# Storing the high and low part of each activation piece side by side, with every high part at a multiple of 256 bytes

## The chip, the cores and the metric

The kernel runs on one core of a Trainium2 chip. Its time is the device time of that core in microseconds (us), as the median of several executions. A profile is one further execution, recorded by the hardware. In it PE is TensorE's matmuls, PEld TensorE's weight loads, DVE is VectorE, ACT is ScalarE, POOL is GpSimd and SP is SyncE. All times are us unless marked ns.

## The reference, cut to what matters

The kernel is one step of an encoder with two layers over 576 tokens (512 of a prompt and 64 of a running stream) of width 1024. Each layer is a SwiGLU feed-forward block, a mixer (pooling in the first layer, an mLSTM in the second) and another feed-forward block:

```python
def _swiglu(u, w_in, w_out):
    h = u @ w_in
    a, b = h[..., :D_FF], h[..., D_FF:]          # D_FF = 2816
    return (jax.nn.silu(a) * b) @ w_out

x = x + 0.5 * _swiglu(_rmsnorm(x, norm_ffn1[i]), ffn1_w_in[i], ffn1_w_out[i])
x = x + mixer(_rmsnorm(x, norm_mix[i]))          # pooling or mLSTM
x = x + 0.5 * _swiglu(_rmsnorm(x, norm_ffn2[i]), ffn2_w_in[i], ffn2_w_out[i])
```

All data is float32. Everything that the change touches is the operand `u` of `u @ w_in`.

## The kernel before, in words

**Precision.** A float32 matmul is done as three passes of fp32r matmuls: each operand is split into a high part (rounded to fp32r) and a low part (the rest), and `passes` (line 1822) gives weight high x data high, weight high x data low, weight low x data high. The weight is the stationary operand and is loaded anew for each matmul, the data is the moving operand of 288 columns (`HALF`, half of the tokens), and so 288 x 4 = 1,152 bytes of each partition are streamed.

**Products.** `u @ w_in` is computed by a Strassen-like scheme with seven products M1 to M7 for each of 11 pairs of output tiles, in each of the two phases of each of the four feed-forward blocks ffn_a to ffn_d. Each product has one of seven combinations of quarters of u as its data. They lie in `u7[kp, part, piece]` with four contraction tiles kp, two parts (high, low) and seven pieces. `PIECES` and `MOVING` (lines 40 to 41) give the piece: M1 has piece 0, M5 1, M2 2, M3 3, M7 4, M6 5 and M4 6. `product_mm` (line 1835) issues one product, here called a **unit**: 4 kp x 3 passes = 12 matmuls in a row on PE, always in the order high, low, high of the data (and weight high, high, low). `product_orders` (line 44) is the order in which PE takes the units; from pair 3 on it repeats M1, M5, M4, M6, M2, M3, M7. `product_waits` puts two semaphore waits ahead of each unit. In the first phase of a block, the first units are interleaved kp by kp.

**Addresses.** A partition's memory is laid out by a running pointer, `region` (line 142). In this build x starts at byte 16,512, which is 128 above a multiple of 256, and takes 72 x 256 bytes, so that `u7` starts at 128 above a multiple of 256 as well. A piece is 1,152 bytes, 4.5 x 256. So in the kernel before a high part starts 128 above a multiple of 256 where its piece is even (M1, M2, M7, M4) and at a multiple of 256 where it is odd (M5, M3, M6), and its low part, seven pieces further, lies the other way round. Below these are the **128-first** and the **0-first** units. The weights `w_hi` and `w_lo` start 128 above a multiple of 256, and each weight tile is 2 x 256 bytes. The `h` tiles (the hidden layer, data of the output product, line 1832) start at a multiple of 256, the second half of the tokens 1,152 bytes behind the first.

**Who fills u7.** ACT writes each high part (`u7_high`, line 754) from a float32 copy (`stage`), in three groups of pieces (`PARTS`: 0 to 1, 2 to 3, 4 to 6), and DVE the low part by a subtraction (`u7_low`, line 1272). ACT also splits all weights (`hi`, line 688, L721), and DVE makes their low part (L1223).

**The place where u7 meets something else.** In the mLSTM the mixer's data `um_hi` and `um_lo` lie in the last 36,864 bytes of u7's region. The output projection of the mixer reads them tile by tile; during its last tile, PE counts `u_free` up after each of seven contraction steps. `u7_high` of ffn_d for kp 2 and 3 therefore waits for `u_free`, and DVE's low parts of kp 1 too (line 1758).

Of the kernel before, what the change touches and what calls it, by code (L numbers as in the profile page):

```python
# [3 lines left out]
P = 128  # L4
D_MODEL = 1024
DT = D_MODEL // P
KP = DT // 2
SEQ, DEC_SEQ = 512, 64
TOK = SEQ + DEC_SEQ
HALF = TOK // 2  # L10
# [121 lines left out]
U_POOL, U_M, U_MOUT, U_END = AT["pool", 0], AT["gates",], AT["mout", 0], len(KEYS)  # L132


def encoder_step(nc, a):
    F32, F32R = mybir.dt.float32, mybir.dt.float32r
    ALU, ACT = mybir.AluOpType, mybir.ActivationFunctionType


    place = [(nc.sbuf_base + 63) // 64 * 64]  # L140

    def region(size):
        offset = place[0]
        place[0] += (size + 63) // 64 * 64
        assert place[0] <= nc.sbuf_usable_end, place[0]
        return offset

    def sb(name, shape, dt=F32, at=None):
        size = 4
        for s in shape[1:]:  # L150
            size *= s
        return nc.alloc_sbuf_tensor_at(name, shape, dt, offset=region(size) if at is None else at)

    x = sb("x", [P, DT, TOK])


    u_at = region(KP * 2 * 7 * HALF * 4)
    u7 = sb("u7", [P, KP, 2, 7, HALF], F32R, at=u_at)
    up_at = u_at + KP * 2 * 7 * HALF * 4 - 2 * DT * U_STRIDE * 4
    up_hi = sb("up_hi", [P, DT, U_STRIDE], F32R, at=up_at)  # L160
    up_lo = sb("up_lo", [P, DT, U_STRIDE], F32R, at=up_at + DT * U_STRIDE * 4)
# [103 lines left out]
    def halves(ap):  # L265
        return ap.rearrange("p (h n) -> p h n", h=2)

    def f32(ap):
        return ap.bitcast(F32)
# [24 lines left out]
    hi_split, lo_split, unit_used = sem("hi_split"), sem("lo_split"), sem("unit_used")  # L294
# [124 lines left out]
    with block as block:  # L419
# [255 lines left out]
        def _(act):  # L675
# [78 lines left out]
            def u7_high(f, kp, part):  # L754

                if part == 1:
                    act.activation(u7[:, kp, 0, 2:4, :], halves(x[:, 2 * kp + 1, :]), ACT.Copy,
                                   scale=ngains[:, f.norm, 2 * kp + 1:2 * kp + 2]).then_inc(u7_hi[1], 1)
                    return
                act.wait_ge(sums_made[part // 2], KP * f.i + kp + 1)  # L760
                first, end = PARTS[part]
                src = stage(f, kp)[:, first:end, :] if part else even_stage(f, kp)
                act.activation(u7[:, kp, 0, first:end, :], src, ACT.Copy) \
                    .then_inc(u7_hi[part], 1)

            def square_tile(j):
# [347 lines left out]
            def mix_square(j):  # L1114

                act.wait_ge(x_ready, 5 * DT + j + 1)
                if j == 0:
                    act.wait_ge(norm_psum, 5)
                elif j > 1:
                    act.wait_ge(mix_added, j - 1)  # L1120
                act.activation((sq if j else sumsq)[:, :], x[:, j, :], ACT.Square).then_inc(mix_squared, 1)

            for j in range(DT - 1):
                ahead(U_MOUT + j)
                act.wait_ge(x_ready, 5 * DT + j + 1)
                if j % 2 == 0:
                    negs_even(ffn_d, j // 2)
                else:
                    negs_odd(ffn_d, j // 2)
                if j in (1, 3):  # L1130
                    for part in range(3):
                        u7_high(ffn_d, j // 2, part)
                mix_square(j)
            act.wait_ge(u_free, 4)
            u7_high(ffn_d, 2, 0)
            u7_high(ffn_d, 2, 1)
            u7_high(ffn_d, 3, 0)
            act.wait_ge(u_free, 6)
            u7_high(ffn_d, 2, 2)
            upto(ffn_d.unit(0, "M7", 0))  # L1140
            act.wait_ge(x_ready, 6 * DT)
# [54 lines left out]
        def _(dve):  # L1196
# [75 lines left out]
            def u7_low(f, kp, part):  # L1272

                dve.wait_ge(u7_hi[part], KP * f.i + kp + 1)
                first, end = PARTS[part]
                src = stage(f, kp)[:, first:end, :] if part else even_stage(f, kp)
                dve.tensor_tensor(u7[:, kp, 1, first:end, :], src,  # L1277
                                  f32(u7[:, kp, 0, first:end, :]), ALU.subtract).then_inc(u7_made[part], 1)

            def add_last(norm):  # L1280

# [540 lines left out]
        def _(pe):  # L1822
            def passes(u, kk, m_h, m_l):

                w = slice(PLACE[u] + kk * P, PLACE[u] + (kk + 1) * P)
                return (w_hi[:, w], m_h), (w_hi[:, w], m_l), (w_lo[:, w], m_h)
# [9 lines left out]
            def product_mm(f, ph, prod, n, kp):  # L1836

                u = f.unit(ph, prod, n)
                dst = r_bank(n) if prod in ("M5", "M3") else q_bank(f, ph, n) if prod == "M2" else p_bank(n)
                piece = PIECES.index(MOVING[prod])  # L1840
                for p, (w, m) in enumerate(passes(u, kp, u7[:, kp, 0, piece, :], u7[:, kp, 1, piece, :])):
                    mm = pe.matmul(dst, w, m, start=prod in ("M1", "M2", "M5") and kp == 0 and p == 0,  # L1842
                                   stop=kp == KP - 1 and p == 2,
                                   skip_group_check=prod in ("M3", "M4", "M6", "M7"))
                if kp == KP - 1:
                    mm.then_inc(unit_used, 1)
# [510 lines left out]
```

## Time and profile before

| | |
|---|---|
| time, median of 3 runs | 1896.24 (1896.02 to 1899.24) |
| span of the profiled execution (first to last instruction) | 1892.5 |
| what lies around the span, taken against the median | 3.7 |
| PE busy | 1871.9 (99% of the span) |
| DVE, ACT, POOL busy | 1254.4, 869.7, 329.9 |
| matmuls on PE | 13,850 |
| of these with u7 as data (L1842) | 7,392 |
| mean granted TensorE clock, share of full speed | 0.997 |

The profiled execution's own time is not recorded apart from its span; the 3.7 us are the difference to the median of the runs, the start and the end of the program. A matmul's duration in the profile, 297 ns, is its time through the pipeline; matmuls overlap, and what counts is the distance between the starts of two neighbours, some 132 to 134 ns.

### The profile page before, as it was taken

The numbers are of one execution on the slowest core, as the hardware profiler recorded it, in microseconds if no ns is written. First come the engines' busy times: TensorE is split into PE (matmuls) and PEld (weight loads), VectorE is DVE, ScalarE is ACT, GpSimd is POOL, SyncE is SP. The second block draws the span as 40 slices with busy tenths as digits, with TensorE's granted clock in tenths as the row PEclk, the third lists the DMA queues.
The fourth block names the chain that finished last, engine by engine and source line by source line (L and its number), as shares of the span: only waits on it lengthen the run. The fifth ranks groups of instructions, "written<-read, shape, count | busy, mean of one in ns | idle before, by whom it ended". The sixth has DMA issues, their size and how long they took to land.

```text
span 1892.5 us, 34440 instructions
## 1 busy us (share of the span) xinstructions
PE 1871.9 (99%) x13850; PEld 1851.5 (98%) x13850; DVE 1254.4 (66%) x1999; ACT 869.7 (46%) x1518; POOL 329.9 (17%) x352
## 2 busy tenths in 40 slices
PE   8999999999999999999999999999999999999998
PEld 8999999998999999999999999999989999999998
DVE  7874487668874488678853786463446888448843
ACT  7652355347652355345532553232434665235532
POOL 2220122121220122132201221300010322012112
PEclk9999999999999999999999999999999999999999
DMA  8773576324773576347644763221113576357632
GB/s 208 162 151 102 125 165 151 107 86 96 161 154 99 125 165 151 106 102 167 144 131 101 171 142 96 90 100 68 57 45 107 118 173 145 102 122 166 130 93 81
DMA packets 116831, 234.71 MB, mean 124 GB/s; under 512 B 13185, under 2 KB 15249, under 8 KB 116673
## 3 DMA queue, kind: packets, MB, share of 16 engines
q1 hardware_dynamic: 77440, 160.59, 27.8%
q0 software_dynamic: 38208, 69.42, 22.3%
q8 instruction: 111, 1.82, 0.4%
q10 hardware_dynamic: 1024, 2.49, 0.4%
q14 instruction: 48, 0.39, 0.1%
HBM read 228.92 MB, written 3.53 MB: 123 GB/s over the span
## 4 chain that ended last, share of the span: by engine, by line
PE 93%; DVE 4%; ACT 2%; DMA 1%; issue 1%; DVEq 0%; ACTq 0%
PE ps L1842 49%; PE ps L1832 39%; DVE w_lo L1223 1%; PE ps L1887 1%; DMA raw_y<-in_ffn_in 1%; PE ps L2159 1%; PE ps L2225 0%; DVE u L1277 0%; PE ps L2162 0%; DMA x<-in_x 0%; PE ps L2024 0%; PE ps L2149 0%; ACT w_hi L721 0%; DVE rstd L1294 0%; PE ps L2134 0%
## 5 line engine op out<-in xcount | busy, mean ns | idle before, releaser
L1842 PE MATMUL ps<-u,w_hi 128*128 128x288 f32 x4928 | 991.9, 297 | 9.5 <-DVE w_lo L1223 4.5
L1842 PEld LDWEIGHTS ps<-u,w_hi 128*128 128x128 f32 x4928 | 794.5, 189 | 13.9 <-DVE w_lo L1223 6.8
L1842 PE MATMUL ps<-u,w_lo 128*128 128x288 f32 x2464 | 729.5, 296 | 0.0
L1842 PEld LDWEIGHTS ps<-u,w_lo 128*128 128x128 f32 x2464 | 464.1, 188 | 0.0
L1832 PE MATMUL ps<-h_lo,w_hi 128*128 128x288 f32 x1386 | 297.9, 296 | 0.0
L1832 PE MATMUL ps<-h_hi,w_hi 128*128 128x288 f32 x1386 | 297.8, 296 | 0.0
L1832 PE MATMUL ps<-h_hi,w_lo 128*128 128x288 f32 x1386 | 297.8, 296 | 0.0
L721 ACT ACTIVATE w_hi<-w_raw 128x768 fp32r<-128x768 f32 (+3 forms) x164 | 136.4, 838 | 319.4 <-PE ps L1832 255.7
L1223 DVE TENSOR_TENSOR w_lo<-w_raw,w_hi 128x768 fp32r<-128x768 f32 (+3 forms) x164 | 167.9, 1032 | 164.2 <-ACT w_hi L721 162.0
L1832 PEld LDWEIGHTS ps<-h_hi,w_hi 128*128 128x128 f32 x1386 | 223.1, 189 | 0.0
L1832 PEld LDWEIGHTS ps<-h_hi,w_lo 128*128 128x128 f32 x1386 | 222.8, 189 | 0.0
L1832 PEld LDWEIGHTS ps<-h_lo,w_hi 128*128 128x128 f32 x1386 | 222.7, 189 | 0.0
L583 POOL DMA_DIRECT2D raw_y<-in_ffn_in x88 | 76.1, 872 | 805.6 <-DVE raw_z L1229 797.6
L721 ACT ACTIVATE w_hi<-raw_y 128x512 fp32r<-128x512 f32 x176 | 110.2, 633 | 181.0 <-PE ps L1842 87.3
L721 ACT ACTIVATE w_hi<-raw_z 128x512 fp32r<-128x512 f32 x176 | 111.2, 633 | 109.1 <-PE ps L1842 68.2
L1223 DVE TENSOR_TENSOR w_lo<-raw_z,w_hi 128x512 fp32r<-128x512 f32 x176 | 121.2, 689 | 51.0 <-ACT w_hi L721 50.2
L1223 DVE TENSOR_TENSOR w_lo<-raw_y,w_hi 128x512 fp32r<-128x512 f32 x176 | 122.9, 700 | 40.9 <-ACT w_hi L721 34.8
L1223 DVE TENSOR_TENSOR w_lo<-raw_a,w_hi 128x512 fp32r<-128x512 f32 x132 | 90.9, 688 | 36.1 <-ACT w_hi L721 36.1
L1832 PE MATMUL ps<-um_hi,w_hi 128*128 128x288 f32 x512 | 113.8, 304 | 0.6 <-DVE q_t L1576 0.4
L575 POOL DMA_DIRECT2D raw_x<-in_ffn_in x88 | 94.5, 1074 | 97.6 <-DMA raw_x<-in_ffn_in 96.3
L1832 PE MATMUL ps<-um_hi,w_lo 128*128 128x288 f32 x512 | 109.6, 296 | 0.0
L1832 PE MATMUL ps<-um_lo,w_hi 128*128 128x288 f32 x512 | 109.5, 295 | 0.0
(268 smaller groups left out, 2125.1 us busy)
## 6 DMA issues: line engine op xcount, KB each, us to landing
raw_a<-in_ffn_in SPq DMA_DIRECT2D x132, 256.0 KB, 4.2
w_raw<-in_ffn_out SPq DMA_DIRECT2D x64, 384.0 KB, 3.1
raw_y<-in_ffn_in SPq DMA_DIRECT2D x88, 256.0 KB, 3.6
raw_x<-in_ffn_in SPq DMA_DIRECT2D x88, 256.0 KB, 2.6
raw_x<-in_ffn_in POOLq DMA_DIRECT2D x88, 256.0 KB, 6.4
raw_y<-in_ffn_in POOLq DMA_DIRECT2D x88, 256.0 KB, 4.9
raw_z<-in_ffn_in POOLq DMA_DIRECT2D x88, 256.0 KB, 4.9
w_raw<-in_ffn_out SPq DMA_DIRECT2D x64, 320.0 KB, 3.0
```

What stands on the lines that cost most here:

```text
L575: pool.dma_start(raw_x[g % 2][:, :], f.w_in[ph * PAIRS + n, 3, :, :], accum_op=ALU.add) \
L583: pool.dma_start(raw_y[g % 2][:, :], f.w_in[ph * PAIRS + n, 2, :, :], accum_op=ALU.add) \
L721: act.activation(w_hi[:, PLACE[u]:PLACE[u] + cols], src, ACT.Copy).then_inc(hi_split, 1)
L1223: dve.tensor_tensor(w_lo[:, PLACE[u]:PLACE[u] + cols], src, f32(w_hi[:, PLACE[u]:PLACE[u] + cols]), ALU.subtract).then_inc(lo_split, 1)
L1832: mm = pe.matmul(ps[:, bank + h, 0:HALF], w, m[:, h * HALF:(h + 1) * HALF], start=first and p == 0, stop=last and p == 2)
L1842: mm = pe.matmul(dst, w, m, start=prod in ("M1", "M2", "M5") and kp == 0 and p == 0, stop=kp == KP - 1 and p == 2, skip_group_check=prod i ...
L1887: mm = pe.matmul(ps[:, 6 + h, 0:HALF], mean_w[:, :], sq8[:, j, h * HALF:(h + 1) * HALF], start=i == 0, stop=i == DT - 1, skip_group_check= ...
L2159: mm = pe.matmul(ps[0:L, 4 + h, 0:DV + 1], probs[0:L, h, c0:c0 + L], v_one[0:L, c, h, :], start=True, stop=c == 0)
```

## The change

`u7` becomes `[kp, piece, part]`, so that a piece's high and low part lie side by side: 2 x 1,152 = 9 x 256 bytes for each piece. The region is moved up by 128 bytes to a multiple of 256. Every high part of all seven pieces then starts at a multiple of 256, and every low part 128 above one. A second `align` moves the next region (raw weights, and with it all that follows) to 128 above a multiple of 256, which is its residue before; in all it moves up by 256 bytes. The `um` and `up` tiles (data of the mixers), which end with u7's region, move up by 128 bytes.

With the new layout other parts of u7 share memory with `um`, so ACT's writes for ffn_d are put in another order with other waits.

```diff
+    def align(size, residue=0):
+        place[0] += (residue - place[0]) % size
+
+    align(256)
+    u_at = region(KP * 7 * 2 * HALF * 4)
+    u7 = sb("u7", [P, KP, 7, 2, HALF], F32R, at=u_at)
+    align(256, 128)
...
-                act.activation(u7[:, kp, 0, first:end, :], src, ACT.Copy) \
+                act.activation(u7[:, kp, first:end, 0, :], src, ACT.Copy) \
...
-                    for part in range(3):
+                    for part in range(3 - j // 2):
                         u7_high(ffn_d, j // 2, part)
                 mix_square(j)
+            act.wait_ge(u_free, 2)
+            u7_high(ffn_d, 1, 2)
             act.wait_ge(u_free, 4)
             u7_high(ffn_d, 2, 0)
-            u7_high(ffn_d, 2, 1)
             u7_high(ffn_d, 3, 0)
             act.wait_ge(u_free, 6)
+            u7_high(ffn_d, 2, 1)
+            act.wait_ge(unit_used, U_MOUT + DT)
             u7_high(ffn_d, 2, 2)
...
-                dve.tensor_tensor(u7[:, kp, 1, first:end, :], src,
-                                  f32(u7[:, kp, 0, first:end, :]), ALU.subtract).then_inc(u7_made[part], 1)
+                dve.tensor_tensor(u7[:, kp, first:end, 1, :], src,
+                                  f32(u7[:, kp, first:end, 0, :]), ALU.subtract).then_inc(u7_made[part], 1)
...
-                for p, (w, m) in enumerate(passes(u, kp, u7[:, kp, 0, piece, :], u7[:, kp, 1, piece, :])):
+                for p, (w, m) in enumerate(passes(u, kp, u7[:, kp, piece, 0, :], u7[:, kp, piece, 1, :])):
```

The order of instructions on PE, DVE, POOL and SP is the same as before; only ACT's differs, at the end of the mLSTM. There, on ACT, before (u_50 is u7, stage_76 the float32 pieces of kp 1; x_ready counts the residual's tiles):

```order
L751 ACTIVATE stage_76<-x,ngains 128x576 [waits x_ready]
L763 ACTIVATE u_50<-stage_76 128x576 [waits sums_even_made]
L757 ACTIVATE u_50<-x,ngains 128x576
L763 ACTIVATE u_50<-stage_76 128x864 [waits sums_odd_made]
L1121 ACTIVATE sq<-x 128x576 [waits mix_added,x_ready]
L721 ACTIVATE w_hi<-raw_y_61 128x512 [waits unit_used,a11_landed0]
```

And now:

```order
L756 ACTIVATE stage_76<-x,ngains 128x576 [waits x_ready]
L768 ACTIVATE u_50<-stage_76 128x2x288 [waits sums_even_made]
L762 ACTIVATE u_50<-x,ngains 128x2x288
L1126 ACTIVATE sq<-x 128x576 [waits mix_added,x_ready]
L726 ACTIVATE w_hi<-raw_y_61 128x512 [waits unit_used,a11_landed0]
```

The write of the last three pieces of kp 1 (128x864) has left this place. A little later on ACT, during the projection's last tile, before (stage_77 and stage_78 are kp 2 and 3):

```order
L1121 ACTIVATE sq<-x 128x576 [waits mix_added,x_ready]
L763 ACTIVATE u_50<-stage_77 128x576 [waits sums_even_made,u_free]
L757 ACTIVATE u_50<-x,ngains 128x576
L763 ACTIVATE u_50<-stage_78 128x576 [waits sums_even_made]
L763 ACTIVATE u_50<-stage_77 128x864 [waits sums_odd_made,u_free]
```

And now:

```order
L1126 ACTIVATE sq<-x 128x576 [waits mix_added,x_ready]
L768 ACTIVATE u_50<-stage_76 128x3x288 [waits sums_odd_made,u_free]
L768 ACTIVATE u_50<-stage_77 128x2x288 [waits sums_even_made,u_free]
L768 ACTIVATE u_50<-stage_78 128x2x288 [waits sums_even_made]
L762 ACTIVATE u_50<-x,ngains 128x2x288 [waits u_free]
L768 ACTIVATE u_50<-stage_77 128x3x288 [waits sums_odd_made,unit_used]
L726 ACTIVATE w_hi<-raw_y_61 128x512 [waits unit_used,s3_summed0]
```

The write for kp 1 stands here now, two writes for kp 2 and 3 have changed places, and the last write of kp 2 waits for the end of the whole projection (unit_used) where it waited for its sixth step. Behind it stands the split of the weight of M7.

## Rows read from the trace of the kernel before

**Rows 1.** The page: busy time, share of the span and instructions of each engine.

```profile
PE 1871.9 (99%) x13850; PEld 1851.5 (98%) x13850; DVE 1254.4 (66%) x1999; ACT 869.7 (46%) x1518; POOL 329.9 (17%) x352
```

**Rows 2.** The page: the chain that ended last, by engine and line.

```profile
PE 93%; DVE 4%; ACT 2%; DMA 1%; issue 1%; DVEq 0%; ACTq 0%
PE ps L1842 49%; PE ps L1832 39%; DVE w_lo L1223 1%; PE ps L1887 1%; DMA raw_y<-in_ffn_in 1%; PE ps L2159 1%; PE ps L2225 0%; DVE u L1277 0%; PE ps L2162 0%; DMA x<-in_x 0%; PE ps L2024 0%; PE ps L2149 0%; ACT w_hi L721 0%; DVE rstd L1294 0%; PE ps L2134 0%
```

**Rows 3.** Groups of PE instructions: count, busy us, mean ns, idle before.

```profile
L1842 PE MATMUL ps<-u,w_hi 128*128 128x288 f32 x4928 | 991.9, 297 | 9.5 <-DVE w_lo L1223 4.5 <-DVE u L1277 3.5 <-ACT side L799 0.7
L1842 PE MATMUL ps<-u,w_lo 128*128 128x288 f32 x2464 | 729.5, 296 | 0.0
```

**Rows 4.** PE's waits: who released it, us in total, times, longest.

```profile
PE ps L1842 <- DVE w_lo L1223: 4.5, 2, 3.2
PE ps L1842 <- DVE u L1277: 3.5, 4, 1.9
```

**Rows 5.** Timeline of PE, ffn_b, second phase, units' first matmuls: start, us.

```profile
644.68 0.29 PE L1842 MATMUL ps<-u,w_hi 128*128 128x288 f32 x1
...
646.30 0.29 PE L1842 MATMUL ps<-u,w_hi 128*128 128x288 f32 x1
...
647.88 0.29 PE L1842 MATMUL ps<-u,w_hi 128*128 128x288 f32 x1
...
649.50 0.30 PE L1842 MATMUL ps<-u,w_hi 128*128 128x288 f32 x1
...
651.09 0.30 PE L1842 MATMUL ps<-u,w_hi 128*128 128x288 f32 x1
...
652.67 0.29 PE L1842 MATMUL ps<-u,w_hi 128*128 128x288 f32 x1
...
654.29 0.30 PE L1842 MATMUL ps<-u,w_hi 128*128 128x288 f32 x1
...
655.88 0.30 PE L1842 MATMUL ps<-u,w_hi 128*128 128x288 f32 x1
...
657.46 0.43 PE L1842 MATMUL ps<-u,w_hi 128*128 128x288 f32 x2
...
659.05 0.42 PE L1842 MATMUL ps<-u,w_hi 128*128 128x288 f32 x2
...
660.66 0.43 PE L1842 MATMUL ps<-u,w_hi 128*128 128x288 f32 x2
```

**Rows 6.** Windows of L1842: stretch, us, PE and PEld busy (count), clock, DMA.

```profile
675.05:764.54 89.49, 89.49 (x674) 89.49 (x673) 1.00 0.69 155
```

**Rows 7.** Windows of L1832 (data h) in ffn_b's second output product.

```profile
767.80:838.10 70.30, 70.30 (x528) 70.26 (x527) 1.00 0.33 93
```

**Rows 8.** Windows, all engines: mLSTM's output projection, then ffn_d's four interleaved units.

```profile
1448.98:1492.45 43.47, 43.47 (x325) 43.31 (x325) 32.85 (x42) 23.48 (x35) 12.99 (x12) 1.00 0.36 94
1492.45:1498.85 6.40, 6.40 (x50) 6.33 (x48) 6.13 (x11) 4.33 (x8) 1.02 (x2) 1.00 0.99 177
```

**Rows 9.** PE at the pooling projection (up is its stationary operand): durations min/median/max.

```profile
L2024 PE MATMUL ps<-w_hi,up_hi x40: 278/281/367, 412.6 to 433.6; 128*128 128x256 f32 x32, 128*79 128x256 f32 x8
```

**Rows 10.** Timeline of ACT at the mLSTM's end: start, us, [idle before, releaser].

```profile
1473.05 0.93 ACT L763 ACTIVATE u<-stage 128x864 fp32r<-128x864 f32 x1 [0.18 <-DVE stage L1269]
...
1487.80 0.67 ACT L1121 ACTIVATE sq<-x 128x576 f32<-128x576 f32 x1
1489.45 0.69 ACT L763 ACTIVATE u<-stage 128x576 fp32r<-128x576 f32 x1 [0.98 <-PE ps L1832]
1490.04 0.77 ACT L757 ACTIVATE u<-x,ngains 128x576 fp32r<-128x576 f32 x1
1490.71 1.50 ACT L763 ACTIVATE u<-stage 128x576 fp32r<-128x576 f32 x2
1493.74 0.64 ACT L721 ACTIVATE w_hi<-raw_y 128x512 fp32r<-128x512 f32 x1 [1.54 <-DMA raw_y<-in_ffn_in]
```

**Rows 11.** Timeline of DVE in the same stretch.

```profile
1488.62 2.95 DVE L1277 TENSOR_TENSOR u<-stage,u 128x576 fp32r<-128x576 f32 x2
1492.65 0.76 DVE L1744 TENSOR_TENSOR x<-x,ps 128x576 f32<-128x576 f32 x1 [1.08 <-PE ps L1832]
...
1495.93 0.51 DVE L1265 SCALAR_TENSOR_TENSOR stage<-x,gains,stage 128x288 f32<-128x288 f32 x1
```

More of the change, by code:

```diff
@@ L154, in encoder_step @@
     x = sb("x", [P, DT, TOK])
-    u_at = region(KP * 2 * 7 * HALF * 4)
-    u7 = sb("u7", [P, KP, 2, 7, HALF], F32R, at=u_at)
+    def align(size, residue=0):
[4 more added lines that the diff above has]
+    align(256, 128)
     up_at = u_at + KP * 2 * 7 * HALF * 4 - 2 * DT * U_STRIDE * 4
@@ L756, in u7_high @@
                 if part == 1:
-                    act.activation(u7[:, kp, 0, 2:4, :], halves(x[:, 2 * kp + 1, :]), ACT.Copy,
+                    act.activation(u7[:, kp, 2:4, 0, :], halves(x[:, 2 * kp + 1, :]), ACT.Copy,
                                    scale=ngains[:, f.norm, 2 * kp + 1:2 * kp + 2]).then_inc(u7_hi[1], 1)
```

## The prediction, written before the changed kernel ran

> **What bounds the kernel.** I read the page first. PE is busy for 1871.9 of 1892.5 us [rows 1], and the chain of what ended last runs through PE for 93%: 49% in L1842, the products on u7, and 39% in L1832 [rows 2]. The reader is to see that nothing but PE's own pace is worth much: the whole idle time ahead of L1842's matmuls is 9.5 us [rows 3], and of it only 3.5 us in four waits are for u7 itself [rows 4]. So a change of u7's addresses can act in two ways: on the distance between two matmuls, or on these few waits.
>
> The next view is therefore the timeline of PE, read not by durations (all are 290 to 300 ns) but by the starts of the units. All stand in one stretch without a wait, in the second phase of ffn_b, where the order is M1, M5, M1, M5, M6, M2, M7, M2, M6, M4, M3. The starts are 649.50 (M5), 651.09 (M6), 652.67 (M2), 654.29 (M7), 655.88 (M2), 657.46 (M6), 659.05 (M4) and 660.66 (M3) [rows 5]. So the lengths are:
> - M5 and M6, 0-first units, the second of them behind another 0-first one: 652.67 - 649.50 = 3.17, or 1.585 each.
> - M2 behind M6, a 128-first unit behind a 0-first one: 1.62.
> - M7 behind M2 and M2 behind M7, 128-first behind 128-first: 657.46 - 654.29 = 3.17, 1.585 each.
> - M6 behind M2, 0-first behind 128-first: 1.59.
> - M4 behind M6, 128-first behind 0-first again: 1.61.
>
> The same product, M2, takes 1.62 behind M6 and 1.58 behind M7, with the same PSUM bank to leave and to enter in both cases (M6 and M7 write the same kind of bank). The number of instructions and waits is the same too. What differs is where the data of the unit before ended: M6's last pass reads a high part at a multiple of 256 bytes, M7's one at 128. Three of the four successions run at the fast pace; only 0-first followed by 128-first is slow.
>
> The sizes to one more digit: the five fast units above take 3.17 + 4.76 (654.29 to 659.05) = 7.93, 1.586 each. From M1 of pair 3 at 675.05 to M3 of the last pair at 764.54 there are eight repetitions of the seven units M1, M5, M4, M6, M2, M3, M7 in 89.49 us [rows 6] (672 starts; the count of 674 has two that were still running). One repetition is 11.186. In it M4 (behind M5), M2 (behind M6) and M7 (behind M3) are slow and four units fast: (11.186 - 4 x 1.586) / 3 = 1.614. A slow unit costs 0.028 us more, 12 matmuls at 134.5 ns instead of 132.2.
>
> **The change, part by part.**
>
> *The products.* With all high parts at multiples of 256, every unit is a 0-first one behind a 0-first one. The succession is in the trace (M6 at 651.09, fast). Slow units before: in a second phase M1 of pair 1, M2 and M4 of pair 0, M7 and M4 and M2 and M7 around pairs 1 and 2 (7), 3 in each of the 8 further repetitions (24) and the last M4: 32, times four blocks = 128. In the first phases, where the head differs and other matmuls stand between some units, I count 31, 30, 29 and 29 = 119. Together 247. Gain 247 x 0.028 = 6.9 us.
>
> *The heads.* The first unit of a second phase, behind the h tiles, takes 646.30 - 644.68 = 1.62 [rows 5]; as a 0-first unit I take it at 1.586, 4 x 0.03 = 0.1. The four units that ffn_c and ffn_d interleave alternate strictly between the two residues and take 6.40 us for 48 matmuls, 133.3 ns each [rows 8] (the count of 50 again has two running ones); at 132.2 they gain 0.05 each, 0.1 together.
>
> *The mixer's data.* um moves by 128 bytes, so its first half goes from 128 to 0 and its second from 0 to 128. Its matmuls alternate between the residues in both cases. Before, with the 128 first, they run 43.47 us / 326 = 133.3 ns [rows 8]; h, with the 0 first, runs at 70.30 / 528 = 133.1 to 133.3 [rows 7]. That is the same pace, so I take nothing, with 1,568 x 0.2 ns = 0.3 us to either side. up moves too, as stationary operand of 120 matmuls [rows 9]; the largest difference known here is that of a slow and a fast matmul, 2.3 ns, so 0.3 us to either side and 0 in the sum.
>
> *The residue of what lies above.* All of it moves by 256 bytes and keeps its residue to 256. Within the trace, data tiles lie at 0 and at 256 above multiples of 512 in turn (h from one k to the next), and h's pace of 133.3 is one number; so I take 0. No row has the weights in another place.
>
> *Strided writes.* DVE and ACT now write runs of 288 with a gap. The trace has DVE reading in two pieces (L1744, 0.76 for 576 elements), which costs no more than the continuous subtraction; a strided write it does not have. A tenth more on ACT's and DVE's some 0.75 us each [rows 10, 11], with about six such instructions ahead of each of the four blocks, would be 0.45 us each, 1.8 us, if PE waited for all of it; below nothing there is no reason. The waits for u7 are only 3.5 us in four [rows 4], so I take 0 and keep 1.8 for the range.
>
> *The new order on ACT.* Removed at 1473.05: 0.93 us [rows 10]; ACT then waits elsewhere. It comes back behind the square at 1487.80, so from 1488.5 to 1489.4. Step four of the last projection was seen at 1489.45 (the start of the write that waited for it), so kp 2's first write starts there as before, kp 3's at 1490.04, the next (0.77) when step six is done, at about 1489.45 + 2 x 0.80 = 1491.05, and the last, 0.93 long, at the end of the projection. That end is seen by DVE at 1492.65 [rows 11]. So ACT is free at 1493.6, and the split of M7's weight behind it waited for a DMA until 1493.74: 0.1 us of slack. DVE's kp 1 subtractions start at 1488.62 and end at 1491.57; the second needs ACT's write of 1489.4 and has it in time. DVE's next use of ACT's late work is the 1495.93 row. What is late by x there reaches PE only beyond 1 us. Cost 0, upper bound 1 us.
>
> **Sum.** 6.9 + 0.1 + 0.1 = 7.1. Against the profiled execution, 1892.5 becomes 1885.4; its start and end around the span stay at 3.7, so the median goes from 1896.24 to **1889.1**. Own range: the slow unit's excess may be 0.025 to 0.031 by the rounding of the rows (6.2 to 7.7), unknown costs up to 3: 1887.5 to 1892.4.
>
> **Two rules of the Trainium skill.** The trace has the same product at 1.58 and at 1.62 us. The page "SBUF — State Buffer", section "Who interferes with whom", gives PE two independent read ports, one for the moving operand and one for weight loads, and says "PE and ACT never wait on anyone". By it no address could change PE's pace, and the change would give 0; the trace disagrees with the first half of that in the kernel before. The fastest long pace here is 132.2 ns. The page "TensorE: Matmul & The Clock Gate", section "Back-to-back issue gap", gives N / 2.4 + 2.5 ns, an estimate of 122.5 for 288 columns; no stretch here shows it, and if the new layout reached it for all 7,392 matmuls the gain would be some 80 us.
>
> **The rivals.**
> 1. *No change.* The slow units are slow by their place in the order, not by addresses: M4, M2 and M7 of the repetition stay at 1.614, and the time stays at 1896.2. For it: the longer units there are always the same three products. Against it: M7 and M2 at the head, in another succession, are fast. The page above on SBUF stands on this side.
> 2. *A still faster pace.* The first M5 behind M1 takes 647.88 - 646.30 = 1.58 [rows 5], by rounding 1.57 to 1.59; if it is 1.575, a pace better than 1.586 exists, and if a run of 0-first units settled in it, all 616 units would gain another 0.011, 6.8 us: 1882.3. Against it: M6 behind M5, 0-first behind 0-first as all will be, is at 1.58 to 1.59 [rows 5].
> 3. *Slower.* What is carried from unit to unit is a phase between weight loads and data, and an unbroken run of 0-first units, or the weights 256 bytes higher, keeps the bad one. Then all units take 1.614: the 369 shorter units lose 0.028 each, +10.3, 1906.6. It decides as soon as more units are lengthened to 1.614 than the 247 that are mended. Against it: the passes within a 0-first unit are the same as before, and its entry from another one was fast.
> 4. *Half.* ACT's or DVE's later work eats 3 us or more of the gain: 1892.5.
>
> **How the numbers follow.** Forecast 0.76, no change 0.06, still faster 0.08, slower 0.05, half 0.05. A difference under 0.2% (3.8 us) can't be told from no change; the forecast with its costs is beyond that but for a small part. Faster 0.87, within 0.2% 0.08, slower 0.05. The range takes the forecast's own and reaches down towards the still faster pace: 1885.5 to 1892.5.
>
> **What would show it.** In the new trace every unit's start is 1.586 us behind the last, a repetition of seven takes 11.10 instead of 11.19, and M4, M2 and M7 are as long as the others. The phases of ffn_a to ffn_d shrink by 0.8 to 0.9 each. h and um stay at 133.3 ns. Around the mLSTM's end PE has no wait over 0.5 us. It is wrong if M4 still takes 1.61 (rival 1) or if M5 does (rival 3), or if PE waits for u at ffn_d's start.

## The result, and the profile after

The changed kernel takes 1879.04 us (median of 4 runs, 1878.1 to 1880.99), the kernel before 1896.3 in the same session (4 runs, 1896.02 to 1899.24). The ratio is 0.9908, 95% interval 0.9896 to 0.992. It is faster as forecast, but by 17.3 us where 7.1 were forecast, and below the range given. The profiled execution has a span of 1878.1 and a time of 1879.91, so 1.8 us lie around the span. The 3.7 us that stand for this before the prediction compare the span of one execution with the median of others: with 1.8 us around it, the profiled execution of the kernel before took some 1894.3 us, 2 below that median, and the profiled one of the kernel after is 0.9 above its own. That is why the span has lost only 14.4 us against [rows 1], and the median 17.3.

The page of the kernel after, busy time of the engines, and the groups of PE instructions (count, busy us, mean ns, idle before), which answer to [rows 1, 3]. The last line is the output product's group in the kernel before:

```profile
PE 1855.2 (99%) x13850; PEld 1834.6 (98%) x13850; DVE 1251.5 (67%) x1999; ACT 866.9 (46%) x1518; POOL 329.5 (18%) x352
...
L1850 PE MATMUL ps<-u,w_hi 128*128 128x288 f32 x4928 | 984.0, 295 | 11.7 <-DVE w_lo L1231 4.5
...
L1850 PE MATMUL ps<-u,w_lo 128*128 128x288 f32 x2464 | 727.1, 295 | 0.0
...
L1840 PE MATMUL ps<-h_hi,w_hi 128*128 128x288 f32 x1386 | 294.4, 293 | 0.0
...
L1832 PE MATMUL ps<-h_hi,w_hi 128*128 128x288 f32 x1386 | 297.8, 296 | 0.0
```

PE is still the bound, and its count is the same. L1850 (u) has lost 1 to 2 ns per matmul, as meant. But L1840 (h, the output product), which the change doesn't touch, has lost 3 of its 296.

The products first. Windows of L1850 (stretch, us, PE busy and count, clock, DMA): from M1 of pair 3 to the last M3, in ffn_b's second phase, which answers to [rows 6], and in ffn_c's first:

```profile
669.76:758.61 88.85, 88.85 (x674) 1.00 0.72 157
863.76:951.88 88.12, 88.12 (x675) 1.00 0.73 160
```

56 units take 88.85 where they took 89.49: 1.587 each, M4, M2 and M7 like the others. Over all phases, from pair 3 to the end, 200 units of the kernel before are longer than 1.60 us, as the prediction's count has it (25 in each phase), and in the kernel after only two, both beside a wait. In ffn_c's first phase the same 56 units take 1.573 each, in the same code and at the same addresses. Below, a product phase is a **132.2 phase** or a **131.1 phase**, by its ns per matmul.

Now the output products. Windows of the kernel before, 60 us (the last 58) inside each of the eight:

```profile
150.00:210.00 60.00, 60.00 (x453) 1.00 0.30 89
344.00:404.00 60.00, 60.00 (x452) 1.00 0.32 94
576.00:636.00 60.00, 60.00 (x452) 1.00 0.30 87
769.00:829.00 60.00, 60.00 (x452) 1.00 0.30 89
965.00:1025.00 60.00, 60.00 (x452) 1.00 0.30 87
1158.00:1218.00 60.00, 60.00 (x452) 1.00 0.31 91
1619.00:1679.00 60.00, 60.00 (x452) 1.00 0.30 88
1812.00:1870.00 58.00, 58.00 (x437) 1.00 0.27 79
```

And of the kernel after:

```profile
148.00:208.00 60.00, 59.98 (x462) 1.00 0.32 97
340.00:400.00 60.00, 60.00 (x453) 1.00 0.34 99
571.00:631.00 60.00, 60.00 (x462) 1.00 0.32 97
762.00:822.00 60.00, 60.00 (x464) 1.00 0.32 96
955.00:1015.00 60.00, 59.98 (x451) 1.00 0.32 97
1148.00:1208.00 60.00, 60.00 (x463) 1.00 0.33 98
1607.00:1667.00 60.00, 59.81 (x461) 1.00 0.32 97
1798.00:1856.00 58.00, 58.00 (x447) 1.00 0.30 87
```

Before, every stretch holds 452 or 453 (437 in the 58 us); after, six hold 9 to 12 more (a count can be one or two off) and two hold 451 and 453. There is nothing between. By the starts, a tile of 66 matmuls (11 contraction steps, three passes, two halves of the tokens; an output product has eight tiles) takes 8.80 us in the first kind and 8.58 in the second. In the first the distances repeat every four matmuls, as 131, 132, 140, 131 ns; in the second they alternate between 132 and 128. I call these the **133 pattern** and the **130 pattern**, by their means (133.3 and 130.0).

The sums of all distances from one start on PE to the next, by what the matmul reads as data, in us:

| | before | after | difference |
|---|---|---|---|
| u (7,392 matmuls) | 1002.3 | 996.8 | -5.5 |
| h (4,224, with the 66 of the last tile) | 563.4 | 553.1 | -10.3 |
| um (1,568) | 215.9 | 217.4 | +1.5 |
| all others | 103.5 | 103.3 | -0.2 |

The 5.5 of u are a gain of 7.7 in pace, of which 2.2 went into longer waits (by the page's idle time ahead of L1850, 11.7 instead of 9.5). PE's waits, with one that has grown (who was waited for, us in total, times, longest):

```profile
PE ps L1850 <- DVE w_lo L1231: 4.5, 2, 3.2
PE ps L1850 <- DVE u L1285: 3.5, 4, 2.1
PE ps L1850 <- DVE tmp L1325: 1.7, 1, 1.7
```

The third was 0.5 before and sits at the start of ffn_c. The +1.5 of um is one stretch in the mLSTM (all PE):

```profile
1290.00:1293.00 3.00, 3.00 (x21) 1.00 0.00 0
1293.40:1296.70 3.30, 3.30 (x15) 0.50 0.36 118
1297.00:1300.00 3.00, 3.00 (x24) 1.00 0.02 8
```

The granted clock is 0.50 there, its 1.2 GHz level. Ahead of it PE alternated between matmuls on um and matmuls of 4 partitions (L2131), without a pause; 13 distances are 240 ns instead of 133. Before, the same place had 1.00 throughout. It is not due to the change: the profiles of e4 and e6 below, in which all addresses are those of the kernel before, have a stretch at 0.50 in the mLSTM too (um 217.3 in both), and those of e11 to e14, in which the two parts lie side by side, have none there (um 215.8).

### The profile page after: what moved, and what is told of

It reads as the page before. It is cut to its first block, busy times and chain, and to the rows that moved or that the text cites. A ratio compares the mean times of both kernels' runs of the same rounds, so it can differ in the third digit from the quotient of the medians.

```text
span 1878.1 us, 34441 instructions
## 1 busy us (share of the span) xinstructions
PE 1855.2 (99%) x13850; PEld 1834.6 (98%) x13850; DVE 1251.5 (67%) x1999; ACT 866.9 (46%) x1518; POOL 329.5 (18%) x352
## 4 chain that ended last, share of the span: by engine, by line
PE 93%; DVE 4%; ACT 2%; DMA 1%; issue 1%; DVEq 0%; ACTq 0%
PE ps L1850 49%; PE ps L1840 39%; DVE w_lo L1231 1%; PE ps L1895 1%; PE ps L2167 1%; PE ps L2233 0%; DVE u L1285 0%; DMA raw_z<-in_ffn_in 0%; PE ps L2170 0%; DMA x<-in_x 0%; PE ps L2032 0%; PE ps L2157 0%; DVE rstd L1302 0%; ACT w_hi L726 0%; PE ps L2142 0%
## 5 line engine op out<-in xcount | busy, mean ns | idle before, releaser
L1850 PE MATMUL ps<-u,w_hi 128*128 128x288 f32 x4928 | 984.0, 295 | 11.7 <-DVE w_lo L1231 4.5
L1850 PEld LDWEIGHTS ps<-u,w_hi 128*128 128x128 f32 x4928 | 790.6, 188 | 16.4 <-DVE w_lo L1231 9.4
L1850 PE MATMUL ps<-u,w_lo 128*128 128x288 f32 x2464 | 727.1, 295 | 0.0
L1850 PEld LDWEIGHTS ps<-u,w_lo 128*128 128x128 f32 x2464 | 462.6, 188 | 0.0
L1840 PE MATMUL ps<-h_hi,w_hi 128*128 128x288 f32 x1386 | 294.4, 293 | 0.0
L1840 PE MATMUL ps<-h_lo,w_hi 128*128 128x288 f32 x1386 | 294.3, 293 | 0.0
L1840 PE MATMUL ps<-h_hi,w_lo 128*128 128x288 f32 x1386 | 294.3, 293 | 0.0
L1840 PEld LDWEIGHTS ps<-h_hi,w_lo 128*128 128x128 f32 x1386 | 220.4, 188 | 0.0
L1840 PEld LDWEIGHTS ps<-h_hi,w_hi 128*128 128x128 f32 x1386 | 220.3, 188 | 0.0
L1840 PEld LDWEIGHTS ps<-h_lo,w_hi 128*128 128x128 f32 x1386 | 220.3, 188 | 0.0
L1840 PE MATMUL ps<-um_hi,w_hi 128*128 128x288 f32 x512 | 114.8, 305 | 0.6 <-DVE q_t L1584 0.3
L1840 PE MATMUL ps<-um_lo,w_hi 128*128 128x288 f32 x512 | 110.5, 297 | 0.0
L1840 PE MATMUL ps<-um_hi,w_lo 128*128 128x288 f32 x512 | 110.4, 297 | 0.0
```

The lines of the kernel that those rows point to most:

```text
L1840: mm = pe.matmul(ps[:, bank + h, 0:HALF], w, m[:, h * HALF:(h + 1) * HALF], start=first and p == 0, stop=last and p == 2)
```

## The experiments

All of h's gain was unforeseen, so there were three questions: are the products' 5.5 us the predicted mechanism alone; is h's second pace due to the place of the things that moved; and if not, what hands it over? The code of the added matmuls is shown once per kind. Medians are given with their range, ratios against the kernel before in the same session.

**e1, only the place of things above u7.** The kernel before, with

```diff
+    place[0] += 256
     raw_at = region(9 * ENTRY * 4)
```

> The kernel before, with everything that lies above u7 (weights, h, stages) moved up by 256 bytes and u7 left as it was. Theory A (handed-over state: the output product's pace follows from what the products before it left, so the change gained there because its units all are 0-first): all eight output phases stay at 8.80 us a tile, the repetition of seven units at 11.19, time 1896, ratio 1.000. Theory B (place: the weights at another multiple of 256 let the output product run faster): output tiles at 8.58 us in most phases, about 10 us gained there alone, 1886, ratio 0.9945.

Measured: 1895.6 (1892.29 to 1898.84), ratio 0.9994 (0.9984 to 1.0003). The pace of u is as before (the sum, 1006.5 in this profile, has 4 us more of waits), and all eight output products have the 133 pattern. The place of the weights and of h alone is not the cause.

**e2, side by side, but u7 left at 128 above a multiple of 256.** The changed kernel without `align(256)`, so that nothing else moves and all units are 128-first.

> The changed kernel with u7 left at its old start: high and low side by side, but every high part 128 above a multiple of 256, and nothing above u7 moved. All units are 128-first behind 128-first, which the trace before shows at 1.586 us. So the products gain their 6 to 7 us in any theory of mine. Theory A in its simplest form (the residue at which the last unit ends decides: 128 before, 0 in the change): output tiles stay at 8.80 us, time about 1889.5, ratio 0.9965. Theory B (weights in the old place): the same 8.80 and 1889.5. Rival C (equal residues of all units are enough, whichever): output tiles at 8.58 in most phases, time 1879, ratio 0.991.

Measured: 1890.59 (1887.82 to 1891.6), ratio 0.9966 (0.9953 to 0.9979). The first line is its units like [rows 6], the second 60 us of an output product:

```profile
673.62:762.47 88.85, 88.85 (x674) 1.00 0.70 157
```

```profile
768.00:828.00 60.00, 60.00 (x452) 1.00 0.30 87
```

The products' term stands alone here: u 996.7 and h 563.4, a gain of 5.6 in u's sum and 5.6 in the time (1896.15 in that session). What lengthened a unit was standing 128-first behind a 0-first one; which residue all units share does not matter for their pace. e2 also puts the two parts of a piece side by side and has ACT's new order. That these are not what made the units faster rests on [rows 5], where 128-first behind 128-first already runs at 1.585 in the old layout; no run gives all units one residue and keeps the parts apart.

**e3 and e4, the last matmul ahead of the output product.** The changed kernel and the kernel before, with the last three passes of the last unit ordered high, high, low:

```diff
+                both = list(passes(...))
+                if (prod, n) == ("M4", PAIRS - 1) and kp == KP - 1:
+                    both = [both[0], both[2], both[1]]
```

> The changed kernel, but in the very last four-fold step (kp 3) of the last unit of each phase the passes stand as high, high, low, so that PE ends the products with a low part, 128 above a multiple of 256, as before the change. Same matmuls, one pair exchanged eight times. Theory A: all eight output phases at 8.80 us a tile, +10.5 us against the changed kernel, 1889.5, ratio 0.9965 to the kernel before. Theory B: nothing changes, 1879, ratio 0.991.

> The kernel before, with the same exchange in the last kp of the last unit of each phase: PE then ends the products with data at a multiple of 256, as the changed kernel does. Theory A: most output phases at 8.58 us a tile instead of 8.80, up to 14 us gained, 1882 to 1886, ratio 0.993 to 0.995. Theory B: no change, 1896, ratio 1.000.

Measured: e3 1879.11 (1877.16 to 1879.78), ratio 0.9905 (0.989 to 0.992), six of eight output products at 130, though not the same six as in the profile after; e4 1896.77 (1892.32 to 1899.01), ratio 0.9999 (0.999 to 1.0009), none. The residue that the last matmul leaves does not decide. One of e3's six stands behind a 131.1 phase.

**e5, low part first, high part at a multiple of 256 behind it, nothing moved.** u7 stays at its old start, and all units are 0-first by their high parts.

> Side by side with the low part first and the high part second, u7 at its old start and nothing above it moved: high parts at multiples of 256 and low parts 128 above, as in the change, but weights and h exactly where they were before. It differs from e2 only in which of the two parts lies at 0. Theory A2 (after e3 and e4: not the last residue, but the rhythm that a long run of 0-first units leaves decides the output product's pace): 6 or so of 8 output phases at 8.58 us a tile, 1879, ratio 0.991. Theory B2 (0-first units and the weights 256 bytes higher are both needed): all at 8.80, as e2, 1890, ratio 0.9965.

Measured: 1881.31 (1880.64 to 1883.72), ratio 0.9932 (0.9916 to 0.9949). Six of the eight product phases run at 131.1 for most of their length (u 990.9), and only two output products have the 130 pattern, both behind phases that ended at 132.2 (h 559.8):

```profile
572.00:632.00 60.00, 60.00 (x464) 1.00 0.33 95
956.00:1016.00 60.00, 60.00 (x452) 1.00 0.31 90
```

So the move of u7 is not needed either. What the products gain in such a phase the output product behind it does not get.

**e6 and e7, sixteen kinds of added matmuls (none, or one to three of 32 to 288 columns) at the heads of output tiles,** in the kernel before and in the changed one. Their results are overwritten by the tile's own first matmul.

```diff
+                            if k == 0:
+                                for cols, at in GADGETS[(5 * (8 * phase + j) + phase) % 16]:
+                                    pe.matmul(ps[:, out_bank(j), 0:cols], w_hi[...], h_hi[:, 0, at:at + cols],
+                                              start=True, stop=True)
```

> The kernel before with up to three extra matmuls at the head of each output tile (results overwritten), 16 kinds in turn: 288, 256, 224, 192, 160, 144, 64 or 32 columns, data at residue 0 or 128. Theory A2 (the output product has two paces that hold themselves, with unchanged addresses): one kind or another pushes a tile from 8.80 to 8.58 us and the following tiles stay there until another kind pushes back; tiles of both lengths in one run. Theory B2 (the pace is a matter of where things lie): every tile without its extra matmuls takes 8.80. The time itself, 5 to 15 us more, says nothing.

> The changed kernel with the same extra matmuls. Theory A2: the same kinds push between 8.58 and 8.80 as in e6, so that both kernels show the same table of kind and effect. Theory B2: tiles are at 8.58 in all phases but one or two, whatever stands ahead of them.

Measured, one run each: 1905.01 and 1902.53. Both patterns appear in both kernels, in tiles with the same addresses. Behind another tile, a head without an added matmul always keeps that tile's pattern. Most kinds leave or set the 133 pattern. Behind another tile, three (32 or 64 columns from an address at a multiple of 256, 192 columns from 128 above one) set the 130 pattern, but only where the 140-ns distance of the 133 pattern lies 4 matmuls ahead of the head, and never where it lies 2 ahead. Since 66 is not a multiple of 4, tiles alternate between the two positions. Behind the products, 224 columns at the head of a first tile set it once in the kernel before.

**e8, the changed kernel once more.**

> The changed kernel once more, not altered. In its first profile the output phases of ffn_a's second and ffn_c's first half ran at 8.80 us a tile and six at 8.58, and both stood behind a wait of PE in the products. Theory A2: in another execution waits fall elsewhere, so other phases, or another number of them, are at 8.80. Theory B2: the same two phases, since the addresses are the same.

Measured, one run: 1881.81. Of the same program, other output products have the 130 pattern (two, not six), and five product phases are at 131.1 for most of their length instead of one:

```profile
572.00:632.00 60.00, 60.00 (x452) 1.00 0.33 93
762.00:822.00 60.00, 60.00 (x464) 1.00 0.31 91
```

The first line is the third output product, which had 462 in the profile after. So addresses only allow a pattern; something that differs between executions picks it. The traces show where it can act. In ffn_a's second phase the units change their pace at one place late in the phase, and each time at a gap between two units: of 924 ns in the profile after (132.2 to 131.1), 980 in e8 and 256 in e5 (131.1 to 132.2). In e14 there is no more at this place than a distance of 130 ns where the rhythm has 126.

**e9 and e10, one matmul of 32 columns at the head of the second tile of each output product,** in the kernel before and in e2's.

```diff
+                            if j == 1 and k == 0:
+                                pe.matmul(ps[:, out_bank(j), 0:32], w_hi[:, PLACE[u]:PLACE[u] + P],
+                                          h_hi[:, 0, 0:32], start=True, stop=True)
```

> The kernel before with one matmul of 32 columns (data at a multiple of 256 bytes, result overwritten) at the head of the second tile of each output product: 8 matmuls of 13,850. In e6 this kind took the pace from 8.80 to 8.58 us a tile in all four places. Theory A2 (two paces that hold themselves): 54 or 55 tiles at 8.58, the gain 8 x 7 x 0.22 less one = 12 us, all of it in L1832 and none in the products, 1884, ratio 0.9935. If the pace were bound to u7's addresses: 1896, ratio 1.000.

> e2 (side by side, all high parts at 128, u7 and the rest not moved) with the same small matmul at the head of the second tile of each output product. Theory A2: the products' gain of e2 and the output's of e9 add up: 1890.6 - 12 = 1878.5, and it should come out the same in each execution, since e2's entry into the output product was the same in all phases. Ratio 0.9905.

Measured: e9 1885.24 (1883.22 to 1885.56), ratio 0.9936 (0.9921 to 0.995): eight small matmuls make the kernel before 10.6 us faster (1895.79 in that session). u stays at 1002.3, and h falls to 552.2 (page of e9; before, 297.8, 296):

```profile
L1832 PE MATMUL ps<-h_hi,w_hi 128*128 128x288 f32 x1386 | 294.2, 293 | 0.0
```

e10 1890.77 (1885.8 to 1893.16), ratio 0.9968 (0.9955 to 0.9982): the forecast of 1878.5 failed. In its profile four output products went to 130 and four stayed; the four that stayed are those whose first tile had its 140 ns 2 ahead of the second tile's head, by the rule of e6.

**e11, the sixteen kinds ahead of M1 from pair 3 on,** in the changed kernel.

> The changed kernel with the 16 kinds of extra matmuls at the head of M1 in pairs 3 to 10 of each phase. Theory A2: the products' units too have two paces, 1.586 and about 1.573, with the same addresses, and some kind moves them from one to the other; whichever the last pair has at its end decides the output tiles (1.586 gives 8.58, 1.573 gives 8.80). If units depend on their addresses alone, all without extra matmuls take 1.586.

Measured, one run: 1891.86. Units change between 1.587 and 1.573 inside one phase. The four output products at 130 stand behind phases that ended at 132.2, the three behind phases that ended at 131.1 are at 133. A fifth phase ended at 132.2, and its output product is at 133, against the expectation: the pace alone does not decide.

**e12, the rule put to use.** e5's kernel with three small matmuls in the second tile of each output product, and **e15,** the same in the kernel before:

```diff
+                            if j == 1 and k in (0, 3, 7):
+                                at_w = PLACE[u] + kk * P
+                                at_c = 0 if k == 0 else HALF
+                                pe.matmul(ps[:, out_bank(j), at_c:at_c + 32], w_hi[:, at_w:at_w + P],
+                                          h_hi[:, k, 0:32], start=k == 0, stop=k == 0, ...)
```

> This is the kernel of e5 (high and low part side by side, low first, nothing moved, 1881.31) with three more matmuls of 32 columns in the second tile of each output product, ahead of its contraction steps 0, 3 and 7 (the first into columns that the tile then overwrites, the others into columns of the bank that nobody reads). In the traces so far such a matmul took the 4-matmul pattern of an 8.80-us tile to the pace of 8.58 when the pattern's long distance (140 ns) lay 4 matmuls ahead of it, and left or put it at 8.80 when the long distance lay 2 ahead, or when the tile was at 8.58; behind it the long distance lay at a multiple of 4 matmuls from it. By that rule the step of 18 matmuls between the first two takes every state to the same one, and the step of 24 to the third puts that at 8.58. Theory (the pace is a state that each matmul carries on): tiles 3 to 8 of all eight output products at 8.58 whatever the first tile was, h 559.8 -> about 555, three small matmuls at 0.118 us each within that; the time is about 1876.5. Rival (the rule holds only where I read it, at the head of a tile): some output products stay at 8.80, and the small matmuls cost 2.8 us: 1881 to 1885.

> The kernel before with the three matmuls of 32 columns in the second tile of each output product. There every first tile has its long distance 4 ahead of the head (e9). By the rule the first small matmul puts the tile at 8.58, the second takes it back to the 8.80 pattern, and the third to 8.58 again: the second tile shows all three stretches, tiles 3 to 8 are at 8.58, h 563.4 -> 555, the time about 1888. Rival: once at 8.58 it stays there, and the second tile shows one pace only.

Measured: e12 1879.28 (1877.94 to 1884.73), ratio 0.9914 (0.9899 to 0.9929), h 553.9 (forecast 555), tiles 3 to 8 at 8.58 in all eight output products, though the first tiles were at 130 in five, and at 133 in three, in both positions. The time is 2.8 over the forecast. In the profile, of the fastest execution (1877.94), seven product phases ran at 132.2, and u is 995.4, 4.5 more than e5's 990.9. e15 1887.65 in one run, forecast 1888; h 554.5. Its second tile (timeline of PE: start, us; the three stretches are behind the three small matmuls):

```profile
157.18 0.18 PE L1947 MATMUL ps<-h_hi,w_hi 128*128 128x32 f32 x1
...
158.07 0.42 PE L1832 MATMUL ps<-h_hi,w_hi 128*128 128x288 f32 x2
158.33 0.42 PE L1832 MATMUL ps<-h_lo,w_hi 128*128 128x288 f32 x2
...
159.37 0.42 PE L1832 MATMUL ps<-h_hi,w_lo 128*128 128x288 f32 x2
159.63 0.18 PE L1947 MATMUL ps<-h_hi,w_hi 128*128 128x32 f32 x1
...
161.07 0.43 PE L1832 MATMUL ps<-h_hi,w_lo 128*128 128x288 f32 x2
161.33 0.43 PE L1832 MATMUL ps<-h_hi,w_hi 128*128 128x288 f32 x2
...
162.67 0.43 PE L1832 MATMUL ps<-h_hi,w_lo 128*128 128x288 f32 x2
162.93 0.18 PE L1947 MATMUL ps<-h_hi,w_hi 128*128 128x32 f32 x1
...
163.82 0.42 PE L1832 MATMUL ps<-h_hi,w_hi 128*128 128x288 f32 x2
...
165.90 0.42 PE L1832 MATMUL ps<-h_hi,w_lo 128*128 128x288 f32 x2
```

Ten matmuls take 1.30 us in the first stretch (158.07 to 159.37), 12 take 1.60 in the second (161.07 to 162.67), and 16 take 2.08 in the third: 130, 133 and 130 ns each. One tile goes through 130, 133 and 130, as the rule says.

**e13 and e14, the units' pace.** The changed kernel with one matmul of 64 columns ahead of M1 of pair 3 (e13), and with e12's three in addition (e14):

```diff
+                        if prod == "M1" and n == 3:
+                            at_w = PLACE[f.unit(ph, prod, n)]
+                            pe.matmul(ps[:, n % 3, 0:64], w_hi[:, at_w:at_w + P], u7[:, 0, 0, 0, 0:64],
+                                      start=True, stop=True)
```

> The changed kernel with one more matmul of 64 columns ahead of M1 of pair 3, in each of the eight product phases. In e11 this kind took the units to 1.573 in four of four places. Theory: all units behind it at 1.573 to 1.574 in all eight phases, u 996.8 -> about 992 (8 x 56 units x 0.0135 = 6.0 less what was at 1.573 before, and 8 x 0.115 for the small matmuls). By the same runs a phase that ends at 1.573 hands the output product a state that leads to 8.80: h 553 -> 563. The sum is 1884 to 1885, slower than the changed kernel although its products are faster. Rival (what the output product gets does not hang on the units' pace): h stays near 553 and the time is 1875.

> The changed kernel with both: the matmul of 64 columns ahead of M1 of pair 3, and the three of 32 columns in the second tile of each output product. Theory: units at 1.573 from pair 3 on (u about 992) and output tiles 3 to 8 at 8.58 in all eight products (h about 555): 1876, where the changed kernel takes 1879.0. Rival (the paces are set by place and chance, not by the matmuls before): no better than 1879, with 3.7 us of small matmuls on top: 1881 to 1883.

Measured: e13 1882.03 (1881.58 to 1884.1), ratio 0.9923 (0.9908 to 0.9938), against 1884 to 1885 forecast. The 64 columns did not do in all phases what they did in e11: two phases stayed at 132.2 behind them and two came back to it, one of these at a gap of 232 ns (u 995.6, not 992). The output products bear out the first theory in part: the four behind phases ending at 131.1 are at 133, and so is one of the others, h 558.1, where 563 was forecast. Its median is 3 us above that of the changed kernel, but the two were measured in different sessions and the intervals of their ratios overlap, so that it is slower is not shown. e14 1879.09 (1878.26 to 1879.2), ratio 0.9904 (0.989 to 0.9918): h 553.7 and all eight output products at 130 from the third tile on, but u 996.2 and nothing won over the changed kernel. No version here beats it clear of the noise.

## Why the prediction was wrong

**Its first step, the units, was right in mechanism and nearly in size.** A 128-first unit behind a 0-first one is longer, and without such successions all take 1.587 or less. e2 has this alone, at 5.6 us; the step and the heads said 7.1. The profile after has 7.7 us of pace in u (0.7 and more of it from the 131.1 phase) and gave 2.2 back in waits, which the forecast had at 0 and allowed up to 3.

**The step that failed is "h and um stay at 133.3 ns", taken from [rows 7] with the words that h's pace is one number.** The term was 0 and it measured 10.3 us, six output products of eight at some 1.7 each. The eight products of the kernel before showed one pace because all eight were entered in the same way, not because there is one. Rival 2 had the right thought, a better pace into which a run of matmuls settles, but gave it only to the units, where it appeared in one phase of eight.

**What decides h's pattern.** e1 and e5 rule out the place of what moved, e3 the last residue, e8 the addresses alone. What remains, and what e12, e14 and e15 force in 24 output products of 24 from whatever entry, is that each pattern hands itself on from matmul to matmul until a matmul of another length interrupts it (in the units, a gap does the same). And the entry comes from the units. Over the profiles with all units 0-first and an unchanged last unit (after, e5, e8, e11 to e14, 56 output products), by how the units' rhythm stands where h begins:

| the units end | output product's first tile | count |
|---|---|---|
| at 132.2, its 137 or 138 and then 126 ns fall on h's first two distances | 8.58 (130) | 27 of 27 |
| at 132.2, the 126 ns is the last distance but one ahead of h | 8.79 (133) | 7 of 7 |
| at 131.1 | 8.77 to 8.80 (133) | 22 of 22 |
| before, e1, e2, e4 (no 125 or 126 ns in the last eight distances ahead of h or h's first two) | 8.78 to 8.81 (133) | 32 of 32 |

So the products' addresses made h faster in an indirect way: in most phases a long run of units of one residue, high part at a multiple of 256, settles into a rhythm in which 126 ns behind 137 or 138 comes back every six matmuls (16% of u's distances are 125 or 126 ns in the profile after, 4% in that of before, none in e2's), and whether h gets the 130 pattern goes with where that rhythm stands at its end. That it is gaps ahead of h that shift it is read from where the pace changes in the traces; no run here puts a gap in on purpose. The table is an observation over many entries; that the last distances are the cause, and not a sign of it, is shown only for the small matmuls inside h. e3, which the table leaves out, warns against reading it as a rule of the pace: there a 131.1 phase led to the 130 pattern. In e3 each of the six entries at 130 has 126 or 125 ns directly ahead of h, and the two at 133 have 131.

**The other steps.** um's pace did not change from its addresses: its last projection takes 43.46 us where [rows 8] had 43.47, and its +1.5 is the clock. Strided writes and ACT's new order: the end of the mLSTM shows nothing. All engines, the last projection and ffn_d's interleaved units, as in [rows 8]:

```profile
1439.58:1483.04 43.46, 43.46 (x325) 43.31 (x325) 32.52 (x42) 22.66 (x34) 13.03 (x12) 1.00 0.35 94
1483.04:1489.42 6.38, 6.38 (x50) 6.23 (x48) 6.10 (x11) 5.24 (x9) 1.03 (x2) 1.00 1.02 183
```

6.38 instead of 6.40: ACT's 5.24 us there, 0.9 more than before, are off the path. The page "SBUF — State Buffer" of the Trainium skill says in the section "Who interferes with whom" that "PE and ACT never wait on anyone". That is said of contention with other engines; the prediction read more into it, that no address could change PE's pace. This wider reading is what e2 refutes: there the addresses of u7 and ACT's order at the end of the mLSTM changed, and PE gained 5.6 us. The 122.5 ns of the page "TensorE: Matmul & The Clock Gate" of the Trainium skill, section "Back-to-back issue gap", come from a formula that the page gives for an isolated matmul, and not for a stream with a weight load for each, as this is. No pattern reached them; the best mean here is 130.0.

The forecast's own range, 1887.5 to 1892.4, is not quite the sum of its terms, which give some 1887.7 to 1892.8; nothing hangs on it.

**The range** let the time be 1885.5 at the lowest. Rival 2 alone stood for 1882.3, at 0.08; a reach to it would still not have held 1879.04.

## What to carry to other kernels

Where PE is the bound, its time is a rhythm of starts: count matmuls in equal stretches of every loop, not of one, and look whether two numbers turn up. Where a group of matmuls is repeated on operands at different addresses, look whether a group gets longer behind one that starts at another residue to 256 bytes, and give all the same (5.6 us here, in e2). And treat "this loop has one pace" as true only for the way it is entered: a change in the loop ahead of it can move it, as can one small matmul (e9), and such a gain can be gone in the next execution of the same program (e8), so compare by several runs.

## What the runs showed of the hardware that I had not expected

- The same 66 matmuls at the same addresses take 8.80 or 8.58 us, and 12 take 1.587 or 1.573, for as long as nothing interrupts them.
- One added matmul of 32 columns costs 0.118 us by itself (31 + 217 ns where 130 stood) and won 1.4 us in each output product of the kernel before.
- The clock stood at 0.50 for 3.3 us in the mLSTM of the profile after, behind matmuls of 4 partitions, and cost 1.5 us; in the profile before it did not, but in those of e4 and e6 it did, with the same addresses as before.
